# Combining the expert outputs of a routed layer: four tiles' rows loaded early, the last two experts added from SBUF

## The reference

```python
h = rms_norm(x, norm_ffn[l]) * (1.0 + sc2) + sh2
# top 1 of 4 groups, then top 2 of 8 experts: eid (T, 2), wts (T, 2)
yb = (silu(xb @ w_gate[e]) * (xb @ w_up[e])) @ w_down[e]      # for the rows xb of each of 32 experts
y = einsum('tkd,tk->td', y_assign, wts)                       # y_assign[t, k]: row of the k-th chosen expert
x = x + g2 * y
out = rms_norm(x, norm_final)
```

## Time and profile before

| | us |
|---|---|
| median of 3 runs | 1715.65 |
| the profiled execution | 1714.84 |
| its span | 1713.1 |
| PE busy | 1612.2 (94%) |
| VectorE (DVE) busy | 1258.1 (73%) |
| ScalarE (ACT) busy | 926.1 (54%) |
| GpSimd (POOL) busy | 307.9 (18%) |

### The profile page before, as it was taken

The page is one execution under the profiler, slowest core; times in us unless marked ns, Lnnn a source line. Parts: engine busy times, 40 slices in busy tenths (PEclk is TensorE's granted clock), DMA queues, the critical chain, the costliest instruction groups (busy, mean ns, idle before and its releaser), DMA issues. The chain is left out here.

```text
span 1713.1 us, 26036 instructions
## 1 busy us (share of the span) xinstructions
PE 1612.2 (94%) x10744; PEld 1408.8 (82%) x10744; DVE 1258.1 (73%) x1496; ACT 926.1 (54%) x1102; POOL 307.9 (18%) x203
## 2 busy tenths in 40 slices
PE   5999999999899999998998995999999999999956
PEld 4899889988898989997997883788888888888842
DVE  5743774377677686865656457899999999999937
ACT  5633244325436353453203123788898888889822
POOL 2410010001101010012000001122334433232230
PEclk9999999999999999999999996999999999999977
DMA  9121013101216233243346326899999999999955
GB/s 334 40 76 39 14 38 118 40 14 38 94 51 190 77 113 105 84 138 127 120 152 213 138 105 263 309 372 389 382 386 392 390 384 381 385 381 398 373 211 224
DMA packets 129552, 345.98 MB, mean 202 GB/s; under 512 B 16369, under 2 KB 72281, under 8 KB 103769
## 3 DMA queue, kind: packets, MB, share of 16 engines
q1 hardware_dynamic: 113704, 312.42, 50.6%
q0 software_dynamic: 9824, 17.88, 2.8%
q10 hardware_dynamic: 5904, 13.99, 2.2%
HBM read 316.16 MB, written 43.81 MB: 210 GB/s over the span
## 5 line engine op out<-in xcount | busy, mean ns | idle before, releaser
L148 PE MATMUL wo_psum_m<-h_hi,x_w_hi 128*128 128x364 f32 (+1 forms) x1184 | 403.6, 341 | 4.6 <-ACT x_x L1030 1.5
L149 PE MATMUL wo_psum_m<-h_lo,x_w_hi 128*128 128x364 f32 (+1 forms) x1184 | 390.3, 330 | 0.0
L150 PE MATMUL wo_psum_m<-h_hi,x_w_lo 128*128 128x364 f32 (+1 forms) x1184 | 390.2, 330 | 0.0
L148 PEld LDWEIGHTS wo_psum_m<-h_hi,x_w_hi 128*128 128x128 f32 x1184 | 223.8, 189 | 17.1 <-issue 7.2
L149 PEld LDWEIGHTS wo_psum_m<-h_lo,x_w_hi 128*128 128x128 f32 x1184 | 223.9, 189 | 2.5
L150 PEld LDWEIGHTS wo_psum_m<-h_hi,x_w_lo 128*128 128x128 f32 x1184 | 223.8, 189 | 0.0
L729 POOL CAST x_w_hi<-x_w 128x1024 fp32r<-128x1024 f32 x44 | 78.3, 1780 | 648.3 <-PE wo_psum_m L150 628.0
L2307 POOL DMA_INDIRECT scratch_y<-e_y,all_tbl x32 | 74.2, 2319 | 374.0 <-ACT e_y L2431 374.0
L1459 DVE TENSOR_TENSOR x_w_lo<-x_w,x_w_hi 128x1024 fp32r<-128x1024 f32 x52 | 64.5, 1241 | 91.0 <-POOL x_w_hi L729 61.8
L1434 DVE TENSOR_REDUCE x_sc<-x_diag 64x64 f32<-64x448 f32 x119 | 110.9, 932 | 1.0
L148 PE MATMUL e_psum_y<-e_d_hi,e_hid_hi 128*128 128x512 f32 x256 | 103.6, 405 | 5.3 <-DVE e_d_lo L2520 5.3
(11 more groups left out here) (389 smaller groups left out, 3647.9 us busy)
## 6 DMA issues: line engine op xcount, KB each, us to landing
mg_ring_hi<-in_w_e_gate SPq DMA_DIRECT2D x34, 1024.0 KB, 10.1
mg_ring_lo<-in_w_e_down SPq DMA_DIRECT2D x34, 1024.0 KB, 8.5
mg_ring_hi<-in_w_e_up SPq DMA_DIRECT2D x32, 1024.0 KB, 8.6
mg_ring_lo<-in_w_e_up SPq DMA_DIRECT2D x32, 1024.0 KB, 8.8
mg_ring_lo<-in_w_e_gate SPq DMA_DIRECT2D x30, 1024.0 KB, 9.9
mg_ring_hi<-in_w_e_down SPq DMA_DIRECT2D x30, 1024.0 KB, 8.7
x_w<-in_w_in SPq DMA_DIRECT2D x44, 512.0 KB, 3.9
scratch_gate<-x_x ACTq DMA_DIRECT2D x16, 544.0 KB, 3.1
```

Source lines behind the costliest of these rows:

```text
L148: nc.tensor.matmul(out, lhs[0], rhs[0], start=start, stop=False)
L149: nc.tensor.matmul(out, lhs[0], rhs[1], start=False, stop=False)
L150: return nc.tensor.matmul(out, lhs[1], rhs[0], start=False, stop=stop)
```

## The change

Five things change, in one edit.

1. **Early rows.** SP loads the `scratch_y` rows of tiles 0 to 3 (`OWNED = 4`) during the last expert, once experts 0 to 29 have been scattered and `u_done` of expert 31 has come; tiles 4 to 8 are loaded after all scatters, as before. The tiles 0 to 3 go to the buffers of the up weights. So that the rows of experts 30 and 31 read as zero there, GpSimd scatters zeros to these rows at the start of the stage (L2372 of the new kernel), between `gather(0)` and `gather(1)`, and waits for them before `gather(1)`, since the zeros lie in its buffer. In the last expert `scatter(30)` waits for the four loads.
2. **Owner matrices.** The rows of experts 30 and 31 (`KEPT = 2`) reach tiles 0 to 3 from the buffer `y` in SBUF: for each of the tiles and experts GpSimd makes a 128x128 matrix that holds, for each slot, the weight at the column of the token that owns it (in expert 17), and PE multiplies with it, accumulating on the tile's diagonal products. For this SP writes the weights `wts` to memory at the start of the stage (L2272, L2273), and GpSimd gathers them by the table (L2378), both before `gather(1)`.
3. **All tiles by PE.** The sums of tiles 0 and 1 move to PE as well; three PSUM areas take turns, in place of two.
4. **Diagonals on ScalarE.** The diagonal matrices are made by ScalarE, tiles 0 to 3 before `keep_y(30)` and tiles 4 to 8 after `hidden_high(31)`.
5. **Down weights in gate buffers.** The down weights of expert 31 are split into the gate weights' buffers, free after the last gate product, in place of `d_hi` and `d_lo`, which are read until `down(30)` ends.

```diff
-        p_g, p_u, p_h = s.psum("g", [P, F]), s.psum("u", [P, F]), s.psum("h", [P, KF, N])
+        p_gu, p_h = s.psum("gu", [P, 2, F]), s.psum("h", [P, KF, N])
+        p_g, p_u = p_gu[:, 0, :], p_gu[:, 1, :]
...
-        ys = s.over("ys", "g_hi", 0, [P, NTT, 2, D])
-        y1, junk = s.over("y1", "d_lo", 0, [P, 3, D]), s.over("junk", "d_lo", 12 * D, [P, D])
-        ALONE = 2
...
+        ys_rows, ys_last, junk = s.over("ys", "u_hi", 0, [P, NT, 2, D]), early["spare"][:, 0:2, :], early["spare"][:, 2, :]
+        ys = [ys_rows[:, t] for t in range(NT)] + [ys_last]
+        OWNED, KEPT = 4, 2
+        owned = [s.over("owned_first", "hot", 0, [P, OWNED // 2, KEPT, P]), s.sb("owned_second", [P, OWNED // 2, KEPT, P])]
+        last_w, last_tok = s.sb("last_w", [P, KEPT]), s.sb("last_tok", [P, KEPT, OWNED])
...
-        sums, diag_ready = [p_x[:, :, :].rearrange("p k n -> p (k n)"), p_y[:, :]], s.sem("diag_ready")
+        sums, diag_ready = [p_x[:, :, :].rearrange("p k n -> p (k n)"), p_gu[:, :, :].rearrange("p a f -> p (a f)"), p_y[:, :]], s.sem("diag_ready")
...
+        def owners(t, i):
+
+            return owned[t // 2][:, t % 2, i, :]
...
+        last_hi, last_lo = (s.over(f"last_{x}", f"g_{x}", 0, [P, KF, D], F32R) for x in ("hi", "lo"))
+
+        def down_halves(e):
+
+            return (last_hi, last_lo) if e == NE - 1 else (d_hi, d_lo)
...
+            sp.wait_ge(router.tiles_counted, 1)
+            wts_rows = wts_d.rearrange("(t k) o -> t (k o)", k=2)
+            sp.dma_start(wts_rows[0:T_PROMPT].rearrange("(t p) k -> p t k", p=P), wts[:, 0:NT, :]).then_inc(wts_out, 16)
+            sp.dma_start(wts_rows[T_PROMPT:T], wts[0:T_SAMPLE, NT, :]).then_inc(wts_out, 16)
...
+            def rows_of_experts(t, sem):
+                t0, n = TILES[t]
+                sp.dma_start(ys[t][0:n], y_rows[t0:t0 + n]).then_inc(sem, 16)
+
+            sp.wait_ge(u_done, NE)
+            sp.wait_ge(last_empty, 16 * KEPT)
+            for b in range(2):
+                sp.wait_ge(y_out[b], arrived(NE // 2 - 2))
+            for t in range(OWNED):
+                rows_of_experts(t, y_in[t])
...
-            sp.wait_ge(combined, 1)
-            for t in range(NTT):
-                t0, n = TILES[t]
-                sp.dma_start(ys[0:n, t], y_rows[t0:t0 + n]).then_inc(y_in[t], 16)
...
+            sp.wait_ge(d_done, NE)
+            for b in range(2):
+                sp.wait_ge(y_out[b], arrived(NE // 2 - 1))
+            for t in range(OWNED, NTT):
+                rows_of_experts(t, y_in[t])
...
+            nc.gpsimd.memset(last_w[:, :], 0.0).then_inc(last_ready, 1)
+            nc.gpsimd.tensor_copy(last_tok[:, :, 0], src[:, NE - KEPT:NE]).then_inc(last_ready, 1)
+            pool.wait_ge(last_ready, 2)
+            for t in range(1, OWNED):
+                nc.gpsimd.tensor_scalar(last_tok[:, :, t], last_tok[:, :, 0], float(t * P), None, ALU.subtract).then_inc(last_ready, 1)
+            for e in range(NE - KEPT, NE):
+                nc.gpsimd.indirect_dma_start(out=y_d, out_offset=bass.IndirectOffsetOnAxis(ap=tbl[:, e:e + 1], axis=0),
+                                             in_=xg[:, 1, :], in_offset=None,
+                                             bounds_check=2 * T - 1, oob_is_err=False).then_inc(last_empty, 16)
+            pool.wait_ge(wts_out, 32)
+            for i in range(KEPT):
+                e = NE - KEPT + i
+                nc.gpsimd.indirect_dma_start(out=last_w[:, i:i + 1], out_offset=None, in_=wts_d,
+                                             in_offset=bass.IndirectOffsetOnAxis(ap=tbl[:, e:e + 1], axis=0),
+                                             bounds_check=2 * T - 1, oob_is_err=False).then_inc(last_in, 16)
+            pool.wait_ge(last_empty, 16 * KEPT)
...
-                if e == NE - 1:
-                    pool.wait_ge(x_turned, NE + 1)
-                    for t in range(ALONE, NTT):
-                        n = TILES[t][1]
-                        for k in range(2):
-                            m = nc.gpsimd.tensor_scalar(diagonal(t)[0:n, k, 0:n], ident[0:n, 0:n], wts[0:n, t, k:k + 1], None, ALU.mult)
-                        m.then_inc(diag_ready, 1)
+                if e == LISTED + NTT:
+                    pool.wait_ge(last_in, 16 * KEPT)
+                    pool.wait_ge(last_ready, OWNED + 1)
+                    for t in range(OWNED):
+                        for i in range(KEPT):
+                            m = nc.gpsimd.tensor_scalar(owners(t, i), consts["slots"], last_tok[:, i, t:t + 1], last_w[:, i:i + 1],
+                                                        ALU.is_equal, ALU.mult)
+                        m.then_inc(owned_ready, 1)
+                if e == NE + 1 - KEPT:
+                    for t in range(OWNED):
+                        pool.wait_ge(y_in[t], 16)
...
+                    if part == "d" and e == NE - 1:
+                        reach(act, g_done, NE)
+                    elif e and half == 0:
                         reach(act, used[part], e)
-                    nc.scalar.activation(his[part][:, half_rows(part, half), :], staged(part, e, half), ACT.Copy).then_inc(hi_done[part], 1)
+                    into = down_halves(e)[0] if part == "d" else his[part]
+                    nc.scalar.activation(into[:, half_rows(part, half), :], staged(part, e, half), ACT.Copy).then_inc(hi_done[part], 1)
...
+            def diagonals(ta, tb):
+
+                for t in range(ta, tb):
+                    n = TILES[t][1]
+                    for k in range(2):
+                        m = nc.scalar.activation(diagonal(t)[0:n, k, 0:n], ident[0:n, 0:n], ACT.Identity, scale=wts[0:n, t, k:k + 1])
+                    m.then_inc(diag_ready, 1)
...
+                else:
+                    high("d", e)
+                if e == NE - 1:
+                    act.wait_ge(x_turned, NE + 1)
+                    diagonals(0, OWNED)
                 if e:
                     keep_y(e - 1)
                 hidden_high(e)
-                high("d", e)
+                if e + 1 < NE:
+                    high("d", e)
+                else:
+                    diagonals(OWNED, NTT)
...
-            def scale_y(t):
-                n = TILES[t][1]
-                act.wait_ge(y_in[t], 16)
-                nc.scalar.activation(y1[0:n, t % 3, :], ys[0:n, t, 0, :], ACT.Copy, scale=wts[0:n, t, 0:1]).then_inc(y_scaled, 1)
...
+                else:
+                    low("d", e)
                 hidden_low(e)
-                low("d", e)
+                if e + 1 < NE:
...
-                if t < ALONE:
-                    dve.wait_ge(y_scaled, t + 1)
-                    V.scalar_tensor_tensor(out=yt, in0=yt, scalar=wts[0:n, t, 1:2], in1=y1[0:n, t % 3, :],
-                                           op0=ALU.mult, op1=ALU.add).then_inc(y_summed, 1)
-                    dve.wait_ge(y_summed, t + 1)
-                    V.tensor_tensor(yt, yt, g2[0:n, g, :], ALU.mult).then_inc(y_gated, 1)
-                else:
-                    dve.wait_ge(sum_done, t + 1 - ALONE)
-                    V.tensor_tensor(yt, sums[t % 2][0:n, :], g2[0:n, g, :], ALU.mult).then_inc(y_gated, 1)
+                yt = ys[t][0:n, 1, :]
+                dve.wait_ge(sum_done, t + 1)
+                V.tensor_tensor(yt, sums[t % 3][0:n, :], g2[0:n, g, :], ALU.mult).then_inc(y_gated, 1)
...
-            for t in range(ALONE, NTT):
+                pe.wait_ge(y_again, 16 * OWNED)
+
+            def weighted(t):
+
                 n = TILES[t][1]
                 pe.wait_ge(y_in[t], 16)
-                pe.wait_ge(diag_ready, t + 1 - ALONE)
-                if t >= ALONE + 2:
-                    pe.wait_ge(y_gated, t - 1)
+                pe.wait_ge(diag_ready, t + 1)
+                if t == 2:
+                    pe.wait_ge(y_kept, NE)
+                if t >= 3:
+                    pe.wait_ge(y_gated, t - 2)
                 for c in (0, HALF):
                     for k in range(2):
-                        m = nc.tensor.matmul(sums[t % 2][0:n, c:c + HALF], diagonal(t)[0:n, k, 0:n], ys[0:n, t, k, c:c + HALF],
-                                             start=(k == 0), stop=(k == 1))
+                        m = nc.tensor.matmul(sums[t % 3][0:n, c:c + HALF], diagonal(t)[0:n, k, 0:n], ys[t][0:n, k, c:c + HALF],
+                                             start=(k == 0), stop=(k == 1 and t >= OWNED))
+                if t >= OWNED:
+                    m.then_inc(sum_done, 1)
+
+            def last_experts(t):
+
+                pe.wait_ge(owned_ready, t + 1)
+                for i in range(KEPT):
+                    pe.wait_ge(y_kept, NE - KEPT + 1 + i)
+                    for c in (0, HALF):
+                        m = nc.tensor.matmul(sums[t % 3][:, c:c + HALF], owners(t, i), y[:, i, c:c + HALF], start=False, stop=(i == KEPT - 1))
                 m.then_inc(sum_done, 1)
+
+            for t in range(OWNED):
+                weighted(t)
+                last_experts(t)
```

(15 more changed lines are left out.)

31 lines of the change are left out of this document (20 added, 11 removed).

## The result

| | before | after |
|---|---|---|
| median of 5 runs, us | 1715.65 | 1725.16 |
| range, us | 1715.21 to 1718.07 | 1724.15 to 1727.18 |
| profiled execution, span, us | 1713.1 | 1722.4 |

The ratio is 1.0053, 95% interval 1.0041 to 1.0064: slower by 0.5%, where I had called 0.2% either way no change. I had forecast 1712.8. Measured once more in another series, the changed kernel stood at 1.0033 (1.0018 to 1.0048) of the kernel before. All ratios here compare fast executions only, and one of the twelve executions of the kernel without TensorE's branch, of 4090.14 us, is left out of its ratio, though not of its median.

What follows compares the result with a forecast made beforehand. PE bounds 31 experts; then a chain of waits ends in VectorE's tail. VectorE's tile 3 earlier (-3.3) and the stage's start (+0.5) give -2.8 on 1714.84: 1712.0, median 1712.8, range 1710.9 to 1717.4.

Steps and rivals of the forecast that it cites:

- down(31): Last expert's down product on PE: starts 1642.55 instead of 1646.00 (-3.45), full clock (-3.1), ends 1648.0 instead of 1654.57.
- The diagonals: ScalarE, eight before keep_y(30): 2.2 to 5.4 us by nearest rows; at 0.4 us each hidden, upper end costs 1.9 us.
- The register and the branch: PE behind down(31), now open: a few tenths to 2.4 us, taken as 1.2; first product at 1649.2.
- the skipped code must be fetched: Rival, 10%: PE's branch costs more than 1.2 us; at GpSimd's bound of 2.4 the sum is -1.6, 1714.0.
- The clock of the first products: Rival, 10%: clock falls at the end, in down(31) (3.1 us) or the first product (3.3); sum +0.3, 1715.9.
- The products: PE's sums: four matmuls per 3.43 us, tiles 0 to 3 twice; tile 3's sum ready at 1676.9.
- nearly cancel: On PE's path, 20.6 us of added products against the load wait of 15.34 and slow first product of 3.3.
- The second load: Rows of tile 4 after the last scatters, at about 1665, needed at 1677: hidden, 12 us to spare.
- The start of the stage: GpSimd's new work ahead of gather(1): issued 1078.3, landing 1083.2 to 1089.2, 1087.0 by one row; +0.5 us.
- The rival: gather(1) holds up the second expert, 22%: weights land late, expert 1 starts nine us late; +5.7, 1721.
- the 8-byte stores: Weights written to memory at the stage's start in 1088 pieces: 10.8 us to landing, dearer if read, modified and written.

Runs made afterwards that it cites:

- the kernel with three edits: Changed kernel with gather(1) directly behind gather(0), weights written behind the first two expert weights loads, register read ahead of down(31): 1715.76 us, 0.9995.

## Why the prediction was wrong

From trace to trace I had forecast -2.8 us, and it came to +9.3. Of these 12.1 us, 6.15 are the start of the stage, 3.74 the stretch up to tile 3, and 2.2 lie ahead of the stage.

*down(31): right.* Forecast 2.5 us after the last hidden turn, all at full clock, ending at 8.0; measured 2.49, and 8.26. The diagonals, guessed at 0.4 us each, took 2.43 us for eight and were hidden. That the clock stays full behind this gap was in part luck: in two of eleven traces with the same gap it didn't. The part's worth in the whole kernel was less than one trace said, 4.8 and 3.9 us in two series.

*The register and the branch: mis-sized.* I took 1.2 us and bounded it by GpSimd's 2.4; it was 3.0, with the packet of code in it. The rival "the skipped code must be fetched" was this mechanism, at a chance of 10% and capped by a row of another engine, whose code is another. +1.8 us.

*The clock of the first products: the step that I had as a rival at 10%.* It fell for part of the first four matmuls, +1.8 us. I had read the clock as safe from one trace in which it stood through 4.3 us of idleness. Behind down(31), gaps of 3.00, 2.89 and 2.99 us lost it and one of 2.76 kept it; but the length of the last gap alone doesn't decide it, since behind the same 1.85 or 1.86 us it fell within down(31) in two traces and stayed in nine.

*The products: right, and the flaw was in what I made of them.* 32 products of tiles 0 to 3, 3.43 us for each four, all rows in time, tile 3's sum when the sum said. I wrote that they "nearly cancel" against the wait they replace, and did not ask whether fewer tiles would be better. Together: tile 3 was forecast 36.97 us after the last hidden turn and came at 40.71; 1.8 + 1.8, and 0.3 from down(31), make it to 0.2 us. (The 3.3 us that I gave to the slow first product of before set a duration, 6.72, against a distance between starts, 3.43; by either measure alone it is 3.1.)

*The second load: right.* Tile 3's rows released scatter(30) at 1663.36, 14.3 us after the last hidden turn; my bound of 1655 was 15.0 after it.

*The start of the stage: the step that failed.* I had +0.5 with gather(1) issued at 1078.3 and landing by 1087. Its weights were ready about then: the second gather of weights ended at 1080.3 in a trace that runs 2.2 us late. What I mis-sized are the zeros. I took them as issued by 1069 and landing in 8.7 to 10.9. The small conversions ahead of them took GpSimd 4.2 us, so that they went out at 1071.04 and 1072.41, and they landed 11.6 and 14.3 us later. So gather(1) went out at 1087.45 and its rows were turned at 1093.91, beyond the landing at 1089.3 from which I had the start decide. The rival priced this at 9 us and blamed the weights; it was the zeros. And one cost was in no part of my sum: the write of the weights delays the rows of gather(0) by 1.4 us and more. Together they cost 6.65 us against 0.5. The two overlap: as long as gather(1) goes out at 1087.45, TensorE waits for its rows however early those of expert 0 come, so the late gather(0) shows only once that wait is gone, with 2.5 and 3.0 us in two runs. Taking away both left nothing (+24.96); the late write without the other edits was not run.

The Trainium skill (DMA: Bandwidth & Descriptors, Specifications) made me fear the 8-byte stores for themselves. They landed in 5.8 and 8.0 us, less than the 10.8 that I took from loads. Where they are issued behind two loads of weights, in the kernel with three edits, they took 10.2 and 14.9 us; GpSimd waited for them, at no cost to the path. No run here shows the read and the write back that it speaks of, and what they cost was the gather beside them.

Left open are the 2.2 us ahead of the stage, which no edit was made to explain. Not settled is what makes the clock fall in one execution and not in another with the same gap, and why the packet of code came 0.7 us ahead of the end of down(31) in two kernels with the early read and 2.0 and 2.2 us ahead of it in the two others.

## What to carry to other kernels

In these runs work that fills a wait paid only up to the wait's length: divide the one by the other before choosing how many tiles to move, and count again what the filler does to what follows. Preparation goes behind the transfers that someone waits for, and a buffer that is soon needed is no source for a store that must land first. A branch that used to lie in a wait has a price once that wait is filled; look for the code packets in the DMA view, and don't bound one engine's branch by another's.

## What the runs showed of the hardware that I had not expected

With a branch on TensorE over a block that isn't entered, the next product started 2.7 to 2.9 us after a packet of code, in eight traces; with neither register read nor branch there was no gap. Such a packet has 16 KB (the page of the kernel before counts 87 in this queue, 1.43 MB). The gap on TensorE was 2.76 to 3.00 us with the register read behind down(31) and 0.69 to 2.13 with it ahead, in four traces each. Two small stores, 0.38 and 0.60 us to issue, made the rows of a gather issued just ahead of them 1.4 to 3.7 us later. Eight 128x128 operations of ScalarE with a scale from SBUF took 2.43 us, 0.30 each:

```profile
1645.48 2.43 ACT L2498 ACTIVATE e_diag<-all_ident,all_wts 128x128 f32<-128x128 f32 x8
```
